# Where the split weights lie in SBUF, modulo 256 bytes, in a two-block transformer kernel on one core

## The reference

```python
# first block, 256 tokens
x = x + parallel_mixer(rmsnorm(x), ...)           # w_in (1024x1992), w_uq, w_ukv, w_out (1024x1024)
x = x + memory_cross_attention(rmsnorm(x), ...)   # wq_x, wkv_x, wo_x
x = x + jnp.square(jax.nn.relu(h @ w_ff1)) @ w_ff2            # 1024x4096 and 4096x1024
# second block, 16 meta tokens in front: 272 tokens
h = h + 0.5 * swiglu(rmsnorm_2(h), gate, up, down)            # 1024x2816 twice, 2816x1024
u = rmsnorm_2(h); ... jnp.split(u @ w_in, offsets)            # 1024x4368
mixed = sigmoid(gate_a) * (ya @ w_branch_att) + sigmoid(gate_b) * (yb @ w_branch_gla)
h = h + mixed @ w_out
h = h + 0.5 * swiglu(rmsnorm_2(h), gate, up, down)            # only the 256 real tokens are kept
return rmsnorm_2(h)[:, N_META:]
```

## Time and profile before

| | |
|---|---|
| median of 3 runs | 943.93 us (943.82 to 945.3) |
| the profiled execution, its own time | 949.94 us |
| its span, first to last instruction | 948.2 us |
| PE busy | 916.9 us (97%) |
| PEld busy | 895.6 us (94%) |
| DVE busy | 652.1 us (69%) |
| ACT busy | 530.5 us (56%) |
| mean granted TensorE clock | 0.996 of full |

### The profile page before, as it was taken

How to read it: one execution, slowest core, us unless ns; L and a number is a source line. 1 busy time by engine, 2 the same in 40 slices (tenths; PEclk the granted TensorE clock), 3 DMA queues, 4 the chain that set the end, 5 groups by cost and what they waited for, 6 DMA issues and landing times.

```text
span 948.2 us, 18496 instructions
## 1 busy us (share of the span) xinstructions
PE 916.9 (97%) x7459; PEld 895.6 (94%) x7459; DVE 652.1 (69%) x1096; ACT 530.5 (56%) x863; POOL 0.2 (0%) x4
## 2 busy tenths in 40 slices
PE   6999999889999999999999999999999999999995
PEld 5898998789999999999999999999999999999995
DVE  7899677677546756766666457687678777777553
ACT  5789867676444645644444345365475565544442
POOL 0000000000000000000000000000000000000000
PEclk9999999999999999999999999999999999999998
DMA  9653234245666556565555554563335556566631
GB/s 288 231 182 123 75 115 149 71 156 187 215 182 183 187 189 193 160 188 174 172 176 175 181 159 134 178 191 101 111 112 158 185 179 214 178 198 201 208 127 45
DMA packets 111172, 157.18 MB, mean 166 GB/s; under 512 B 9696, under 2 KB 62704, under 8 KB 110960
## 3 DMA queue, kind: packets, MB, share of 16 engines
q1 hardware_dynamic: 111088, 156.01, 51.7%
HBM read 154.93 MB, written 1.05 MB: 165 GB/s over the span
## 4 chain that ended last, share of the span: by engine, by line
PE 89%; DVE 5%; ACT 4%; issue 1%; DMA 0%; SPq 0%; DVEq 0%; ACTq 0%
PE ps L983 27%; PE ps L985 27%; PE ps L984 27%; DVE wl L1699 2%; PE ps L1007 1%; ACT wh L1291 1%; PE ps L1040 1%; ACT L1275 1%; DMA raw<-w_in 0%; DVE ACC L1732 0%; ACT U L1370 0%; PE ps L1216 0%; PE ps L1174 0%; PE ps L1236 0%; PE ps L1237 0%
## 5 line engine op out<-in xcount | busy, mean ns | idle before, releaser
L1699 DVE TENSOR_TENSOR wl<-raw,wh 128x1024 fp32r<-128x1024 f32 (+3 forms) x290 | 344.8, 1215 | 185.4 <-ACT wh L1291 184.4
L983 PE MATMUL ps<-U,wh 128*128 128x256 f32 (+2 forms) x1408 | 404.4, 287 | 14.5 <-DVE wl L1699 14.1
L985 PE MATMUL ps<-U,wl 128*128 128x256 f32 (+2 forms) x1408 | 397.5, 282 | 0.0
L1291 ACT ACTIVATE wh<-raw 128x1024 fp32r<-128x1024 f32 (+3 forms) x290 | 295.4, 1047 | 181.1 <-PE ps L985 179.5
L984 PE MATMUL ps<-UL,wh 128*128 128x256 f32 (+2 forms) x1408 | 396.7, 282 | 0.0
L983 PEld LDWEIGHTS ps<-U,wh 128*128 128x128 f32 (+1 forms) x1408 | 263.8, 187 | 18.9 <-DVE wl L1699 15.7
L984 PEld LDWEIGHTS ps<-UL,wh 128*128 128x128 f32 (+1 forms) x1408 | 263.5, 187 | 1.8 <-issue 0.7
L985 PEld LDWEIGHTS ps<-U,wl 128*128 128x128 f32 (+1 forms) x1408 | 264.1, 188 | 0.6
L983 PE MATMUL ps<-H,wh 128*128 128x256 f32 (+1 forms) x736 | 209.2, 284 | 0.1
L985 PE MATMUL ps<-H,wl 128*128 128x256 f32 (+1 forms) x736 | 206.5, 281 | 0.0
L984 PE MATMUL ps<-HLO,wh 128*128 128x256 f32 (+1 forms) x736 | 206.3, 280 | 0.0
(11 more groups left out here) (315 smaller groups left out, 807.3 us busy)
## 6 DMA issues: line engine op xcount, KB each, us to landing
raw<-w_ff SPq DMA_DIRECT2D x64, 512.0 KB, 4.3
raw<-ffn_w_gate SPq DMA_DIRECT2D x88, 256.0 KB, 3.7
raw<-ffn_w_up SPq DMA_DIRECT2D x88, 256.0 KB, 4.5
raw<-ffn_w_down SPq DMA_DIRECT2D x44, 512.0 KB, 4.4
raw<-w_in SPq DMA_DIRECT2D x40, 512.0 KB, 4.3
raw<-w_out SPq DMA_DIRECT2D x16, 512.0 KB, 4.7
raw<-wkv_x SPq DMA_DIRECT2D x8, 512.0 KB, 3.9
raw<-w_in SPq DMA_DIRECT2D x9, 256.0 KB, 3.2
```

Of the source, the lines that this page charges most:

```text
L983: e.matmul(out, sh, xh, start=(i == 0 and n == 0), stop=False)
L985: mm = e.matmul(out, sl, xh, start=False, stop=(over and n == nk - 1))
L1291: e.activation(t["wh"][:, plan.half[v], 0:n], t["raw"][:, v % NRAW, 0:n], ACT.Copy).then_inc(*up("w_hi", v))
L1699: e.tensor_tensor(wl, raw, wh.bitcast(F32), ALU.subtract).then_inc(*up("w_lo", v))
```

## The change

Five tensors change places in the allocation. `RS` (1088 bytes) goes from ahead of `wh` to behind `H`; `gcol` (32 bytes) goes ahead of `wh`; `DC` (32 bytes) goes behind `RM`. `wh` and `wl` so begin 32 bytes above the start of `U` modulo 256, where they began 64 above; `H` and `HLO` stay at 0 and `CQH`/`CQL` at 64. `G` and `RM`, which lie between `wl` and `H`, move with the weights by 32; `RS` and `ACC` come to lie elsewhere as well. The distance becomes 32 for nearly all 256-token matmuls, {32, 224, 160, 96} in turn for the 272-token ones, 224 for `CQH`/`CQL`, and 64 and 96 in "small".

```diff
         t["S"] = sb("S", [P, 13 * SL])
         t["raw"] = sb("raw", [P, NRAW, SLOT])
-        t["RS"] = sb("RS", [P, T2])
-        assert (nc.sbuf_base - base) % 256 == 64
+        t["gcol"] = sb("gcol", [P, 8])
+        assert (nc.sbuf_base - base) % 256 == 32
         t["wh"] = sb("wh", [P, NHL, SLOT], F32R)
         t["wl"] = sb("wl", [P, NHL, SLOT], F32R)
         t["G"] = sb("G", [P, 2, T2])
         t["RM"] = sb("RM", [P, T2])
+        t["DC"] = sb("DC", [P, 8])
         assert (nc.sbuf_base - base) % 256 == 0
         t["H"] = sb("H", [P, 22, T2], F32R)
         top_h = nc.sbuf_base
+        t["RS"] = sb("RS", [P, T2])
         t["ACC"] = sb("ACC", [P, T2])
-        t["gcol"] = sb("gcol", [P, 8])
-        t["DC"] = sb("DC", [P, 8])
         assert (nc.sbuf_base - base) % 256 == 0
         t["HLO"] = sb("HLO", [P, 22, T2], F32R)
```

## The result

The changed kernel takes 962.72 us (median of 4 runs, 962.02 to 962.98), the kernel before 944.62 us beside it on the same chip (943.82 to 946.07). The ratio is 1.0189, with a 95% interval from 1.0171 to 1.0206: slower, by 18.1 us. The direction and the mechanism were forecast. The size was not: 956 was forecast, and the time lies 0.7 us above the range.

The account below looks back on a forecast made before the run. TensorE's pace of starting matmuls was taken to bound the kernel, with at most some 20 us lost by waiting. The median 943.93 plus 11.4 us for 256-token matmuls, all else nothing, gave 955.3, forecast as 956 us; range 935 to 962.

Parts of the forecast that it names:

- The fast pattern is a narrow coincidence which 32 bytes break.: 256-token matmuls: no fast pattern at distance 32; the choice the forecast rests on, around 956 us, chance 0.40.
- The 256-token term: 256-token matmuls, distance 64 to 32: all fast windows lose 4.4 ns per matmul, 9.6 plus 1.8, 11.4 us in all.
- The worst case: 256-token matmuls: the fast pattern doesn't exist at distance 32, fast windows fall to 117.8 ns, costing 11.4 us.
- The other named windows and the estimated 400 matmuls: Fast 256-token windows besides the long one, and fast pieces between gaps ahead of 182 us, the latter put at 1.8 us.
- The 272-token matmuls, taken at nothing: 272-token matmuls: pace stays 125.3 ns at the four new distances, no cost; 1 ns either way, 1.8 us, for the range.
- "Small", the latent products, the vector operations: Fewer than 200 matmuls, at most 1 us, taken at nothing; moved vector tensors carry no price, L1699 stays at 1215 ns.
- the second rival: 256-token stretches: both patterns go on, falling differently after gaps; long stretches worth 5.9 and 6.2 us; 944 to 950 us, chance 0.20.
- Two readings: Profiled 949.94 against median 943.93 us: profiling costs 6 us throughout, or the runs had 206 to 362 us fast, worth 5.9.
- The second reading: Runs had 206 to 362 us at the fast pace, so 1325 more matmuls have it to lose: 961.2 us.
- Easier to enter: Rival for 256-token matmuls: distance 32 is cleaner than 64 and slow stretches vanish; around 938 us, 934 to 942, chance 0.30.
- the draw falls otherwise: The second rival again: distance 32 acts like 64, with fast and slow stretches in other places; 944 to 950 us, chance 0.20.
- the change does nothing: Rival for the whole kernel: weight loads run beside the matmul ahead and distance has no effect; 943.9 us, chance 0.10.

Follow-up runs that it names:

- e3: Kernel before with the weights at distance 32, `RS` left ahead of them and `ACC` behind `H`: 961.59 us, ratio 1.0162.
- e9: Kernel before with weights and streamed tiles both 32 bytes higher, distance still 64: nine runs from 943.8 to 956.8 us, ratio 1.0053.
- e11: Kernel before, block two's first swiglu and down products streaming tile 0 for every k, so one distance (values wrong): one run, 943.0 us.
- e2: Kernel before with weights left at 64, `RS` and `ACC` moved behind `H`, `gcol` ahead of the weights: median 951.26 us, ratio 1.0068.
- e1: The kernel before, unchanged, profiled once more: 947.05 us; twelve other runs on that chip 943.8 to 950.0.
- the seven layouts of the table: Layouts with the weights at distance 0, 32, 48, 64, 96, 128 and 192: 943.93 us at 64, medians of 958.64 to 967.85 us at the others.
- e10: Kernel before plus a kick, three added matmuls at distance 0 at each of four places: median 945.65 us against 945.93, ratio 1.0007.
- e13: Layout of e2 plus the kick of e10: 947.21 us, eight of ten runs from 944.3 to 947.7.
- e14: Layout of e2 plus the same twelve matmuls, streaming the tile due anyway at distance 64: nine of ten runs from 952.1 to 959.6 us.
- e4: Kernel before with `wh` left at 64 and only `wl` at 32, one load in three moved: 963.52 us, ratio 1.0187.
- e7: Kernel before with the weights at distance 0, the place of the streamed tiles: median 967.85 us, ratio 1.0178.

## Why the prediction was right, and where it failed

- **"The fast pattern is a narrow coincidence which 32 bytes break."** Right, for this layout. With 32 no window is fast, e3 shows that `RS` and `ACC` have no part in it, and e9 that it is the distance and not the place. Of the distances tried, 64 is the only one whose long stretches are fast. My picture of a window with the clean spot in the middle was too simple all the same: 192, far off, has the pattern in short stretches.
- **The 256-token term, 11.4 us.** The mechanism was right and the size nearly so, but in part by luck. The profiled executions differ by 962.02 - 949.94 = 12.1 us, which the table of the first section divides. The worst case had taken the slow pace of before, 117.8, and measured was 118.5: the second stretch lost 7.0 us, not 6.2, and the first, already slow, lost 0.7 more. The other named windows and the estimated 400 matmuls had been put at 3.4 + 1.8 = 5.2 us, and gave 1.5 + 0.8 + 1.0 = 3.3, net of shorter waits. Against the 1.9 us that are missing there stand 1.2 us between 194.66 and 206.03, of which the sum knew nothing. They come mainly from the 3.4 us at the lower clock: 15 matmuls at 213.6 ns instead of 118, an estimate of 1.4 us from the two paces, in part given back by a shorter wait.
- **The 272-token matmuls, taken at nothing.** Right: 125.3 became 125.4, which is one record. e11 shows that the distances do cost them 2.1 ns, but the four old ones and the four new ones cost alike.
- **"Small", the latent products, the vector operations.** Right as far as seen: L1699 takes 1216 ns, against 1215 in the earlier trace rows. That moving vector tensors is free was wrong in an indirect way: in e2 it moved no duration, but most runs took as long as with a slow long stretch. The size of this, 6 us, lay in the price of the second rival ("another draw"), which I had given to the distance alone.
- **The step that failed: the base of the sum.** The forecast stood on 943.93 + 11.4, as if the runs had had only the second stretch at the fast pace. "Two readings: the profile costs 6 us throughout, or the runs had the stretch of 206 to 362 us at the fast pace", and I took the first for the forecast. The second is true. e1 is a profiled execution with that stretch fast, at 947.05 us amid other runs and with 2.9 us of it lost to the lower clock; the kernel after took 962.02 when profiled and up to 962.98 when not. Most runs of before so had both long stretches to lose, not the second alone. Profile against profile the loss is 12.1 us, and with the 5.9 of the first stretch it is 18.0, where the medians differ by 18.1. The second reading had given 961.2, and 962.72 is 1.5 above it: 12.1 where 11.4 was taken makes 0.7, and the median run is 0.7 slower than the profiled one, at a mean clock of 0.993 to 0.994 against 0.995. The 6 us lay open in the text, in two equal numbers (5.9 and 6.0) that should have been taken for one.
- **The range.** Its upper edge, 962, was the sum by the second reading with no room for an error of the term. The ±1.8 us that were named for the 272-token pace were not added to it. With them it would have held.
- **The rivals.** "Easier to enter" and "the draw falls otherwise" are both refuted by the missing fast windows, for distance 32; "the change does nothing" by the ratio.

The Trainium skill, "TensorE: Matmul & The Clock Gate", section "Step-by-step: what each phase is for", has it that loading weights doesn't steal read bandwidth from the running matmul. By that the seven layouts of the table would take the same time, and at distance 0 the kernel took 967.85 us where the kernel before took 951.42 in the median on the same chip. The runs don't show whether SBUF, TensorE or something between them causes this; they only show that the distance decides.

## What to carry to other kernels

In a kernel that TensorE bounds, measure the pace, length over matmuls started, in windows without a gap and at one granted clock, before looking at anything else; two paces for one kind of matmul mean that addresses or their order are worth a try, and some 2% lay in 32 bytes here. Read several executions before taking one profile's stretch for the rule: if a profiled time differs from the median by just what one stretch is worth, suspect the stretch before you call it the price of profiling. Read the clock in narrow windows too: 3.4 us at the lower level don't show in the digits of a page. And where a pattern can be missed at a restart, a few matmuls at another distance are a cheap way to get it back (0.35 us for three here), though against the kernel before, on a chip where it drew well, they gained nothing.

## What was not expected of the hardware

- TensorE keeps two or more regular patterns of the same instruction stream, 113.3 and 117.8 ns, each for over a thousand matmuls, at the same granted clock of 1.00 and the same DMA share. Which one a stretch has varies between executions: the same program took from 943.65 to 955.85 us in the runs shown here, of which up to some 3 us can be the clock. The odds differ between chips, too: the kernel before took less than 947 us in 21 of 21 runs on one and in one of seven on another.
- The pattern changes in the middle of a stream where a few matmuls have another distance. Shown by the kick of e10, by the six matmuls at 717 us, and by e13 against e14. What decides it after a gap remains open.
- One load in three at another distance (e4) costs as much as all three, or more: 120.1 ns in the first stretch.
- The distance has a price at the upper clock alone. At the lower level the matmuls start 213.6 ns apart at distance 32 (the kernel after, first section), and just so at 64, in e1, and within 0.2 ns at 0, in e7:

```profile
195.18 0.41 PE L985 MATMUL ps<-U,wl 128*128 128x256 f32 x1
...
200.52 0.38 PE L983 MATMUL ps<-U,wh 128*128 128x256 f32 x1
```

```profile
198.99 0.41 PE L983 MATMUL ps<-U,wh 128*128 128x256 f32 x1
...
201.77 0.41 PE L984 MATMUL ps<-UL,wh 128*128 128x256 f32 x1
```

  These are 25 steps in 5.34 us and 13 in 2.78.
